# Output projection of a hybrid decoder layer: plain float32 matmuls in place of a three-term split

## The reference, cut to what matters

```
merged = (gates[:, :, 0] * (y_sb @ w_sb_out) + gates[:, :, 1] * (y_ssd @ w_ssd_out)
          + gates[:, :, 2] * (y_mem @ w_mem_out))
mix = merged @ w_o                          # 1024 x 1024 by 1024 x 1024
h = h + rms_norm(mix, norm_mix_post)
...
ff = square(relu(u @ w_up)) @ w_down
```

## Time and profile before

| | |
|---|---|
| median of three runs | 3892.03 us |
| span of the profiled execution, first to last instruction | 3885.3 us |
| TensorE matmul busy | 3148.4 us, 81% of the span |
| TensorE weight loads busy | 2503.2 us, 64% |
| VectorE busy | 1917.1 us, 49% |
| GpSimd busy | 1467.2 us, 38% |
| ScalarE busy | 903.4 us, 23% |
| matmuls of the output projection (first start to the copy of the last block) | 2948.50 to 3037.80 us of the span |

### The profile page before, as it was taken

How to read it: one execution, slowest core, us unless ns; L and a number is a source line. 1 busy time by engine, 2 the same in 40 slices (tenths; PEclk the granted TensorE clock), 3 DMA queues, 4 the chain that set the end, 5 groups by cost and what they waited for, 6 DMA issues and landing times. The chain is left out here.

```text
span 3885.3 us, 39604 instructions
## 1 busy us (share of the span) xinstructions
PE 3148.4 (81%) x13740; PEld 2503.2 (64%) x13740; DVE 1917.1 (49%) x1709; ACT 903.4 (23%) x1389; POOL 1467.2 (38%) x824
## 2 busy tenths in 40 slices
PE   5799788888888888777777755589997599999998
PEld 5588566666666666555555643367776477787876
DVE  0300476676767767687787856433331431313123
ACT  3200222222222222333333333221111310101011
POOL 4233344334334334454455520044443043434442
PEclk9799889889889889898888977789998799999998
DMA  3222221121121111222121234243321311111112
GB/s 130 83 97 97 76 76 34 64 76 43 54 76 43 65 68 40 74 70 67 61 71 59 71 114 184 111 176 130 130 81 43 135 60 43 49 43 43 49 43 108
DMA packets 126216, 304.60 MB, mean 78 GB/s; under 512 B 11616, under 2 KB 58336, under 8 KB 126176
## 3 DMA queue, kind: packets, MB, share of 16 engines
q1 hardware_dynamic: 126176, 304.12, 22.3%
HBM read 218.10 MB, written 85.98 MB: 78 GB/s over the span
## 5 line engine op out<-in xcount | busy, mean ns | idle before, releaser
L457 PE MATMUL sb_psg<-uh,sb_wh 128*128 128x512 f32 x768 | 335.4, 437 | 15.0 <-POOL sb_wl L178 15.0
L661 DVE TENSOR_TENSOR_SCAN sb_rest<-sb_keep 128x128 f32<-128x128 f32 (+7 forms) x128 | 337.2, 2635 | 4.4
L592 POOL TENSOR_TENSOR sb_beta<-sb_beta,before 128x128 f32<-128x128 f32 x128 | 78.5, 613 | 681.5 <-ACT sb_beta L554 681.5
L656 DVE TENSOR_SCALAR sb_keep<-sb_beta 128x128 f32<-128x128 f32 (+7 forms) x128 | 185.0, 1445 | 279.5 <-POOL sb_beta L592 278.6
L457 PE MATMUL sb_psg<-ul,sb_wh 128*128 128x512 f32 x768 | 318.7, 415 | 0.0
L457 PE MATMUL sb_psg<-uh,sb_wl 128*128 128x512 f32 x768 | 318.7, 415 | 0.0
L171 POOL TENSOR_TENSOR ff_wh<-ff_w,one 128x1024 fp32r<-128x1024 f32 x64 | 121.2, 1893 | 509.7 <-PE ff_ps L193 417.0
L1441 PE MATMUL mg_ps<-mg_yh,mg_wh 128*128 128x512 f32 x512 | 204.4, 399 | 52.3 <-POOL mg_wl L178 31.6
L171 POOL TENSOR_TENSOR mg_wh<-mg_w,one 128x1024 fp32r<-128x1024 f32 x32 | 62.6, 1957 | 471.9 <-DMA mg_w<-in_w_branch 302.2
L855 PE MATMUL ssd_psg<-uh,sg_wh 128*128 128x512 f32 x384 | 176.3, 459 | 64.2 <-ACT ssd_out L894 64.2
L193 PE MATMUL ff_ps<-ff_fh,ff_wh 128*128 128x512 f32 x512 | 203.5, 397 | 27.3 <-DVE ff_fl L1661 27.3
(11 more groups left out here) (287 smaller groups left out, 8069.6 us busy)
## 6 DMA issues: line engine op xcount, KB each, us to landing
sb_w<-in_w_in SPq DMA_DIRECT2D x49, 512.0 KB, 3.4
scratch_proj<-sb_out SPq DMA_DIRECT2D x48, 512.0 KB, 2.9
mg_raw<-scratch_y SPq DMA_DIRECT2D x32, 512.0 KB, 6.0
mg_w<-in_w_branch SPq DMA_DIRECT2D x32, 512.0 KB, 4.1
mg_gate<-scratch_proj SPq DMA_DIRECT2D x32, 512.0 KB, 3.3
ff_w<-in_w_up SPq DMA_DIRECT2D x32, 512.0 KB, 3.3
ff_w<-in_w_down SPq DMA_DIRECT2D x32, 512.0 KB, 3.3
sb_qkv<-scratch_proj SPq DMA_DIRECT2D x27, 512.0 KB, 5.6
```

The costliest lines, as they stand in the source:

```text
L457: last = nc.tensor.matmul(ps_g[:, h], l[:, s, k], r[:, k, h * HALF:(h + 1) * HALF], start=(k == 0 and j == 0), stop=(k == KB - 1 and j == 2))
L592: nc.gpsimd.tensor_tensor(diag, diag, consts["before"][:], ALU.mult).then_inc(masked, 1)
L656: nc.vector.tensor_scalar(keep[:, 0:cols], beta[:, i % 2, 0:cols], -1.0, 1.0, ALU.mult, ALU.add).then_inc(keep_done, 1)
L661: nc.vector.tensor_tensor_scan(rest[:, i % 2, S - cols:S][:, ::-1], down, down, 1.0, ALU.mult, ALU.bypass).then_inc(scanned, 1)
```

## The change

`split_blocks` goes, with its stage and the tiles `mh` and `ml`. `output_projection` takes the tile `merged` as it is and writes into a new tile `mix`. The weights are used as they are loaded: no split on GpSimd, four slots in place of two. Each product of operands is one matmul with float32 operands in place of three with fp32r operands. The hardware loops give way to straight code, and the number of accumulated terms per PSUM bank falls from 24 to 8.

```
-def split_blocks(nc, name, x, xh, xl):
-            for k in range(KB):
-                nc.scalar.activation(xh[:, k], x[:, k], ACT.Copy).then_inc(hi_done, 1)
...
-                dve.wait_ge(hi_done, k + 1)
-                nc.vector.tensor_tensor(xl[:, k], x[:, k], xh[:, k].bitcast(F32), ALU.subtract)
...
+def output_projection(nc, w_o, merged, mix, consts):
+        DEEP = 4
+        w = ctx.enter_context(nc.sbuf_tensor("wo_w", [P, DEEP, KB, P], F32))
...
+            for n in range(KB):
+                if n >= DEEP:
+                    sp.wait_ge(multiplied, n - DEEP + 1)
+                sp.dma_start(w[:, n % DEEP].rearrange("p k n -> p (k n)"), w_o[n]).then_inc(loaded[n % DEEP], 16)
...
+            for n in range(KB):
+                pe.wait_ge(loaded[n % DEEP], 16 * (n // DEEP + 1))
+                if n >= 2:
+                    pe.wait_ge(evacuated, n - 1)
+                for h in range(2):
+                    cols = slice(h * HALF, (h + 1) * HALF)
+                    for k in range(KB):
+                        last = nc.tensor.matmul(ps[:, n % 2, cols], w[:, n % DEEP, k], merged[:, k, cols],
+                                                start=(k == 0), stop=(k == KB - 1))
+                last.then_inc(multiplied, 1)
...
+            for n in range(KB):
+                act.wait_ge(multiplied, n + 1)
+                nc.scalar.activation(mix[:, n], ps[:, n % 2], ACT.Copy).then_inc(evacuated, 1)
...
-            xh, xl = sb(c, "mh", [P, KB, S], F32R), sb(c, "ml", [P, KB, S], F32R)
-            split_blocks(nc, "ms", merged, xh, xl)
-            output_projection(nc, a["w_o"], xh, xl, merged, consts)
+            mix = sb(c, "mix", [P, KB, S])
+            output_projection(nc, a["w_o"], merged, mix, consts)
```

More of the change, by code:

```diff
@@ L1465, in _ @@
                         nc.vector.tensor_tensor(row, row, gated[:, s], ALU.add).then_inc(summed, 1)
-def split_blocks(nc, name, x, xh, xl):
+def output_projection(nc, w_o, merged, mix, consts):
     with stage(nc) as ctx:
[L1471 to L1475, removed]
-            for k in range(KB):
-                nc.scalar.activation(xh[:, k], x[:, k], ACT.Copy).then_inc(hi_done, 1)
-        @block.vector
-        def _(dve):
-            for k in range(KB):
-                dve.wait_ge(hi_done, k + 1)
-                nc.vector.tensor_tensor(xl[:, k], x[:, k], xh[:, k].bitcast(F32), ALU.subtract)
-def output_projection(nc, w_o, xh, xl, mix, consts):
-    with stage(nc) as ctx:
-        ring = Ring(nc, ctx, "wo", consts)
+        DEEP = 4
+        w = ctx.enter_context(nc.sbuf_tensor("wo_w", [P, DEEP, KB, P], F32))
         ps = ctx.enter_context(nc.psum_tensor("wo_ps", [P, 2, S], F32))
-        evacuated = [nc.alloc_semaphore(f"wo_evac{s}") for s in range(2)]
+        loaded = [nc.alloc_semaphore(f"wo_loaded{s}") for s in range(DEEP)]
+        multiplied = nc.alloc_semaphore("wo_multiplied")
+        evacuated = nc.alloc_semaphore("wo_evacuated")
         block = ctx.enter_context(nc.Block())
@@ L1716, in layer @@
             merge_branches(nc, a["w_branch"], proj, y, merged, consts)
-            xh, xl = sb(c, "mh", [P, KB, S], F32R), sb(c, "ml", [P, KB, S], F32R)
-            split_blocks(nc, "ms", merged, xh, xl)
-            output_projection(nc, a["w_o"], xh, xl, merged, consts)
-            add_normed(nc, "h1", merged, a["norm_mix_post"].broadcast_to([P, D]), a["x"], h, consts)
+            mix = sb(c, "mix", [P, KB, S])
+            output_projection(nc, a["w_o"], merged, mix, consts)
+            add_normed(nc, "h1", mix, a["norm_mix_post"].broadcast_to([P, D]), a["x"], h, consts)
         with ExitStack() as c:
```

## The result

The changed kernel takes 3898.93 us (median of 12 runs, 3892.74 to 3904.96), the kernel before, run beside it, 3891.72 us (12 runs, 3884.8 to 3895.17). The ratio is 1.0019 with a 95% interval of 1.0011 to 1.0028: slower by 7 us, clear of no change, and just inside the 0.2% that the prediction named. Forecast were +7.2 us and 3899.2 us. The prediction took 0.2% as what a measurement can tell from no change; twelve runs of each tell smaller differences apart, with an interval that is 0.17% wide.

A forecast was written before the change was run, and what follows sets the result against it. TensorE was taken to bound the output projection, after a start-up in which it idles. Start-up -16.3 us and body +23.5 us sum to +7.2 us, 3899.2 us; 8 in 10 from 3896 to 3905.5 us.

The forecast's parts named there:

- Start-up: Output projection, merge's end to first matmul: splitting stage and GpSimd's first split go, first matmul 16.3 us earlier.
- Records and their price: Projection's body: 128 float32 matmuls become 256 records of 0.430 us each, 110.1 us at full clock.
- rival 1: Projection's body: each half of a record costs an fp32r matmul, 0.4533 us a record; +13.2 us, 3905.2 us; chance 0.10.
- The clock: Start of the projection's matmuls: TensorE starts cold, 4.4 us at half speed, 2.2 us lost, bounds 1.45 and 3.0.
- Sum: Whole change: -16.3 us of start-up and +23.5 us of body give +7.2 us, 3899.2 us.
- Edits at nothing: Projection: PSUM copies, loads after the first, the `mix` tile and straight code in place of loops cost nothing.
- rival 3: Projection's body: the clock stays at half, 0.853 us a record; +113 us, 4005 us; chance 0.02.
- rival 4: Projection's body: one record of 0.430 us per matmul, body 55 us shorter, 3844 us; chance 0.03.
- Rival 2: Projection's start: first weights come late with four loads in flight, start 2.4 us later; +9.6 us, 3901.6 us; chance 0.08.
- The four passes: Projection's matmuls: the skill's four passes, at one fp32r matmul each, give a 116.1 us body, against 110.1 by the row.
- the forecast's lower end: Low end of the forecast's own range for the whole kernel, 3896.8 us: earliest start, 0.4267 us records, short cold stretch.

The follow-up runs named there:

- the run that kept the clock: Kernel with plain first block, plus 12 fp32r matmuls behind the merge's last and three plain ones at the projection's start; 3878.47 us, ratio 0.9965 to the kernel before.

## Why the prediction was right

- **Start-up.** Predicted 4.4 us from merge to first matmul (0.8 of boundary, 3.6 of load), measured 4.07 (0.86 and 3.21). The load was faster than either row I had taken it from the earlier trace rows. That the term is on the path whole was an argument; putting the stage back showed it: the stage grew by 12.5 us in the trace, 11.3 of them start-up, and the median by 12.2.
- **Records and their price.** 256 records, 0.4292 us each against 0.430 from the earlier trace rows. Here the forecast was decided: at 0.4533 us a record, rival 1, it would have been +13.2 us.
- **The clock.** It starts at half as predicted. I took 4.4 us of it, the trace had 3.5 and the one with the split stage 6.0: it differs from trace to trace, and the upper bound given was 6.0. That it costs half its length is shown twice: the run that kept the clock saved 1.7 us where 3.4 us had been at half clock, and 2.4 us more of it with the stage put back made the body 1.2 us longer.
- **Sum.** The stage went up by 6.0 us, predicted 7.2: 0.3 too long in the start-up and 0.9 in the body, of which about half is the clock, 0.2 the price of the records and the rest the allowance for the two ends. The medians differ by 7.2 us, and the ratio's interval (4 to 11 us) holds both. That the medians meet the forecast to a tenth is luck; 6.0 is what the stage shows.
- **Edits at nothing.** The copies and the later loads are covered: TensorE waits once. Straight code costs nothing in the body; in the start-up about 1 us is in question, which the prediction had in its boundary and load and not under this name. The cover of the loads is thinner than I wrote: a slot comes free three blocks ahead and not four, 41 us before its weights are needed and not 50, which is still over ten times a load.
- **Rivals.** Rival 1 falls by 0.4292, rival 3 by 108 us at clock 1.00, rival 4 by 256 records. Rival 2 falls too: with four loads in flight TensorE started 3.21 us after the issue, so the first was not held up by the others.
- **The four passes.** The Trainium skill ("FP8 and Floating Point Precision", "TensorE Precision Notes") has true float32 as four passes through the array. The trace agrees: 0.858 us a matmul is four times 512 columns at 2.4 GHz and 0.005 more.

By its own terms the forecast's lower end is 3897.3 us and not 3896.8 (16.6 us earlier, a body of 111.2). Another reading was wrong, though no term hung on it. I put the 6.7 us between the profiled span and the median of the runs outside the first and last instruction. Every run that has both figures shows 1.6 to 1.8 us there (3899.12 and 3897.4, for one of the changed kernel). The profiled execution of before was thus itself about 5 us below the median, and a comparison of the two spans would have given 12.1 us for a change of 7.

## What to carry to other kernels

Price an exchange of operand forms by the distance between starts per finished product: here 0.86 us for one plain float32 matmul of 512 columns and 0.68 for three fp32r ones. The plain form loses in the steady state and wins where its operands are ready earlier; here the stage went from 110.0 to 101.6 us by splitting inside it, and from 101.6 to 96.1 by the plain form for the first block alone, beside which the rest is split. Before two elementwise engines are set to work side by side, look at how long each takes when the other is busy.

## What the runs showed of the hardware that I had not expected

VectorE and GpSimd slow each other in float32 passes on 128x1024 tiles: 1.89 to 2.9 us and 2.34 to 3.2 us on GpSimd, and on VectorE from 1.2 us a pass to a mean of 2.1 and single ones of 3.4. The loads in flight do not share evenly: the first of four 512 KB loads was usable after 3.21 us while the slowest took 6.7.

Executions of one kernel scatter by up to 12 us (3892.74 to 3904.96), and what the traces let me place lies in stages that no kernel here touched: in the eleven traces the merge ends between 2927.78 and 2939.01 us, while the way from the last copy's start to the end of the span is always 846.7 to 849.6. A part of it sits in one stretch. From the first load of the memory attention to the first of the merge, the kernel before took 231.0 us and the changed one 234.4:

```profile
L1172 SPq DMA_DIRECT2D ma_gain<-in_ssd_norm x1: 367/367/367, 2292.4 to 2292.4; - x1
L1396 SPq DMA_DIRECT2D mg_raw<-scratch_y x32: 327/328/1000, 2523.4 to 2745.4; - x32
```
```profile
L1172 SPq DMA_DIRECT2D ma_gain<-in_ssd_norm x1: 366/366/366, 2294.5 to 2294.5; - x1
L1396 SPq DMA_DIRECT2D mg_raw<-scratch_y x32: 327/328/727, 2528.9 to 2750.9; - x32
```

Of the nine other traces three have 231.0 to 231.4 us there and six 234.3 to 234.7, with nothing between. Both lengths occur with plain and with three-term matmuls in the projection, so they don't follow the change. Why a stage has two lengths was not tested.
